# Expert weights in one ring of eighteen places, three experts in a loop's body, and waits moved behind the first output stores

## What is computed

```python
logits = xt @ w_router + b_router
top_v, top_e = lax.top_k(logits, 4)
weights = jax.nn.softmax(top_v, axis=-1)
def expert_block(tok, e):
    hcat = x_pad[tok] @ w1[e] + b1[e]                    # w1[e]: 1024 x 2048
    x_glu = jnp.minimum(hcat[:, ::2], 7.0)
    x_lin = jnp.clip(hcat[:, 1::2], -7.0, 7.0)
    act = x_glu * jax.nn.sigmoid(1.702 * x_glu) * (x_lin + 1.0)
    return act @ w2[e] + b2[e]                           # w2[e]: 1024 x 1024
out = sum over a token's four experts of weights * expert_block
```

## Time and profile before

| what | value |
|---|---|
| median of 3 runs | 2680.3 us (2677.91, 2680.3, 2681.9) |
| the profiled execution's own time | 2677.67 us |
| its span, first to last instruction | 2675.9 us |
| PE, DVE, ACT busy | 98%, 42%, 25% of the span |
| queue of SP's and ACT's loads | 664.71 MB of 705.21 MB |
| granted clock of TensorE, mean | 0.999 |

### The profile page before, as it was taken

One profiled execution on the slowest core, in us unless ns is written; L12 is line 12 of the kernel. 1 busy time (PEld: TensorE's weight loads), 2 busy tenths in 40 slices (PEclk: granted clock), 3 DMA queues, 4 the chain that ended last, 5 costly groups with the idle time before them and its releaser, 6 DMA issues.

```text
span 2675.9 us, 37947 instructions
## 1 busy us (share of the span) xinstructions
PE 2620.0 (98%) x15345; PEld 1908.5 (71%) x15345; DVE 1116.0 (42%) x1589; ACT 676.8 (25%) x1201; POOL 73.4 (3%) x95
## 2 busy tenths in 40 slices
PE   7999999999999999999999999999999999999998
PEld 7999888999999998899989888843333333333333
DVE  5866424586587463157823153322122112112212
ACT  3413320342143042213412044122121121112111
POOL 0010200000000120000001000000000000000000
PEclk9999999999999999999999999999999999999999
DMA  6575334456655843334562634779999999999999
GB/s 233 189 263 192 126 126 151 149 173 219 238 174 185 294 164 123 130 142 158 181 206 99 235 130 157 283 291 427 427 428 427 428 428 427 427 428 428 428 427 404
DMA packets 265069, 705.21 MB, mean 264 GB/s; under 512 B 12932, under 2 KB 155216, under 8 KB 214928
## 3 DMA queue, kind: packets, MB, share of 16 engines
q1 hardware_dynamic: 254464, 664.71, 64.5%
q0 software_dynamic: 9856, 36.41, 3.8%
q10 hardware_dynamic: 656, 2.78, 0.3%
HBM read 699.61 MB, written 6.60 MB: 264 GB/s over the span
## 4 chain that ended last, share of the span: by engine, by line
PE 78%; DMA 16%; SPq 4%; DVE 1%; issue 0%; ACT 0%; DVEq 0%; ACTq 0%
PE acc L1005 12%; PE acc L1093 11%; PE acc L1716 7%; PE acc L1050 6%; PE mix L1054 6%; PE acc L1052 6%; DMA ring<-in_w 6%; DMA branch<-in_w 5%; DMA big<-in_w 5%; PE acc L1532 4%; PE mix L1044 4%; PE acc L1731 3%; PE acc L1022 3%; SPq L881 2%; PE acc L1324 2%; SPq L884 2%
## 5 line engine op out<-in xcount | busy, mean ns | idle before, releaser
L1050 PE MATMUL acc<-branch_parts,area_parts 128*128 128x256 f32 x1176 | 344.1, 293 | 0.1
L1054 PE MATMUL mix<-big_parts,zz_parts 128*128 128x256 f32 x1176 | 332.8, 283 | 0.0
L1052 PE MATMUL acc<-area_parts,ring_parts 128*128 128x256 f32 x1176 | 332.4, 283 | 0.0
L1093 PE MATMUL acc<-big,ring 128*128 128x256 f32 (+1 forms) x1408 | 269.7, 353 | 0.0
L1093 PEld LDWEIGHTS acc<-big,ring 128*128 128x128 f32 x1408 | 241.1, 190 | 28.3 <-issue 0.8
L3012 DVE COPY zz<-acc 128x512 f32<-128x512 f32 x32 | 22.1, 691 | 555.9 <-PE acc L1716 555.9
L1050 PEld LDWEIGHTS acc<-branch_parts,area_parts 128*128 128x128 f32 x1176 | 225.0, 191 | 8.9 <-DVE zz_parts L2354 0.5
L1052 PEld LDWEIGHTS acc<-area_parts,ring_parts 128*128 128x128 f32 x1176 | 225.1, 191 | 0.2
L1054 PEld LDWEIGHTS mix<-big_parts,zz_parts 128*128 128x128 f32 x1176 | 225.0, 191 | 0.0
L1005 PE MATMUL acc<-x,ring 128*128 128x256 f32 x1024 | 224.3, 380 | 0.0
L1005 PEld LDWEIGHTS acc<-x,ring 128*128 128x128 f32 x1024 | 193.8, 190 | 26.7 <-issue 0.3
(11 more groups left out here) (506 smaller groups left out, 3667.1 us busy)
## 6 DMA issues: line engine op xcount, KB each, us to landing
big<-in_w SPq DMA_DIRECT2D x129, 1024.0 KB, 25.7
ring<-in_w SPq DMA_DIRECT2D x124, 1024.0 KB, 25.7
ring<-in_ffn_up SPq DMA_DIRECT2D x88, 1024.0 KB, 4.9
ring<-in_w_in SPq DMA_DIRECT2D x72, 1024.0 KB, 7.0
tables<-in_w SPq DMA_DIRECT2D x33, 1024.0 KB, 25.7
branch<-in_w SPq DMA_DIRECT2D x33, 1024.0 KB, 26.0
silu_rope<-in_w SPq DMA_DIRECT2D x31, 1024.0 KB, 25.7
res<-in_w SPq DMA_DIRECT2D x31, 1024.0 KB, 25.4
```

The source lines that it names most:

```text
L1050: pe.matmul(abank(a, b)[:, ts], wg[:, b, k, c * P:c * P + P], xg[:, k, :], start=c == 0 and k == 0, stop=False, skip_group_check=True)
L1052: pe.matmul(abank(a, b)[:, ts], wl[:, k, c0:c0 + P], xl[:, k, :], start=False, stop=k == K - 1, skip_group_check=True)
L1054: mm = pe.matmul(kbank(a, b)[:, ts], wk[:, b, k, c * P:c * P + P], xk[:, k, :], start=False, stop=k == K - 1, skip_group_check=True)
L1093: mm = pe.matmul(outs[c], w[:, k, c * P:c * P + P], rhs(kk), start=opens[c] and kk == 0, stop=kk == FC - 1, skip_group_check=not all(opens))
```

## The change

The constant `NWB` goes from 12 to 18, and unit u now lies in place u mod 18 throughout, so the six additional places are refilled like the others. As 18 places and 12 units an expert meet again only after three experts, the loops over experts 2 to 31 on SP and on PE run ten times over a body of three experts. The wait for the three loads of a next round stands before the fourth store instead of before the first. `first_units` loads all eighteen first units, at the same points in SP's stream as before. The diff's core:

```diff
-NWB = 12
+NWB = 18
...
-        w_landed = [sem(f"w_landed_{n}") for n in range(NWB)]
+        w_landed = [sem(f"w_landed_{n}") for n in range(12)]
...
-        def buffer_of(j):
-            return (8 + j - NX) % NWB
...
+        BUFFERS = tuple((w, 0) for w in w_landed) + \
+            ((small_landed, LAYERS * 176), (apart_landed, LAYERS * 48), (down_landed, LAYERS * 64), (const_landed, 64),
+             (rows_moved, 32), (landed[0], (LAYERS * (RINGED // 2) + 9) * 16))
...
         def laps(n):
-            return 1 + len([u for u in range(NWB + NX, UNITS_Q) if (u - NX) % NWB == n])
...
+            return len(range(n, UNITS_Q, NWB))
...
+        def unit_of(eng, q, u, i=0):
+            sem_n, counted = BUFFERS[u % NWB]
+            eng.wait_ge(sem_n, (q * laps(u % NWB) + 2 * i + (u // NWB + 1)) * 16 + counted)
+            return wbuf[u % NWB]
...
-                spare_units(NWB, NWB + NX - 1)
+                first_units(q, 12, 17)
...
-                spare_units(NWB + NX - 1, NWB + NX)
+                first_units(q, 17, 18)
...
-                def stream(e, first, last):
-
+                def stream(e, u, first, last):
...
                     for j in range(first, last):
-                        turn = NX if isinstance(e, int) and number(e, j) < 2 * NWB + NX else 0
-                        sp.wait_ge(w_used, q * UNITS_Q + e * UNITS_E + (j - 14 - turn))
+                        sp.wait_ge(w_used, q * UNITS_Q + e * UNITS_E + (j - 20))
                         if j < DC:
-                            up_unit(e, j, buffer_of(j))
+                            up_unit(e, j, (u + j) % NWB)
                         else:
-                            down_unit(e - 1, j - DC, buffer_of(j))
-
-                stream(1, 4 + NX, UNITS_E)
-                stream(2, 0, UNITS_E)
-                with sp.Fori(3, EXPERTS) as e:
-                    stream(e, 0, UNITS_E)
+                            down_unit(e - 1, j - DC, (u + j) % NWB)
+
+                stream(1, 8, 10, UNITS_E)
+                with sp.Fori(0, (EXPERTS - 2) // 3) as i:
+                    for d in range(3):
+                        stream(i * 3 + (2 + d), 20 + UNITS_E * d, 0, UNITS_E)
...
-            for n in range(3):
-                sp.wait_ge(w_landed[n], rounds * (16 * laps(n)) + 16)
             for i, n in enumerate((0, 2, 1, 3)):
+                if i == 3:
+                    for m in range(3):
+                        sp.wait_ge(w_landed[m], rounds * (16 * laps(m)) + 16)
                 sp.wait_ge(x_ready, 16 + 48 * LAYERS + 16 + i + 1)
...
-                with pe.Fori(2, EXPERTS) as e:
-                    slots_free(first + e)
-                    up(e, 0, 2)
-                    combine(first + e - 2)
...
+                with pe.Fori(0, (EXPERTS - 2) // 3) as i:
+                    for d in range(3):
+                        e, u = i * 3 + (2 + d), 20 + UNITS_E * d
+                        slots_free(first + e)
+                        up(u, 0, 2, i)
+                        combine(first + e - 2)
...
+                        down_between(e, u + DC, i)
```

More of the change, by code:

```diff
@@ L567, in mixed_blocks @@
         mask_ready = sgu_out
-        w_landed = [sem(f"w_landed_{n}") for n in range(NWB)]
+        w_landed = [sem(f"w_landed_{n}") for n in range(12)]
         w_used = sem("w_used")
[L572 to L580, removed]
-        def buffer_of(j):
-            return (8 + j - NX) % NWB
-        def last_unit(n):
-            return max(u for u in range(NWB + NX, UNITS_Q) if (u - NX) % NWB == n)
-        def laps(n):
-            return 1 + len([u for u in range(NWB + NX, UNITS_Q) if (u - NX) % NWB == n])
[L592 to L604, removed]
+        BUFFERS = tuple((w, 0) for w in w_landed) + \
+            ((small_landed, LAYERS * 176), (apart_landed, LAYERS * 48), (down_landed, LAYERS * 64), (const_landed, 64),
+             (rows_moved, 32), (landed[0], (LAYERS * (RINGED // 2) + 9) * 16))
+        THREE = 3 * UNITS_E
+        def laps(n):
+            return len(range(n, UNITS_Q, NWB))
[3 more added lines that the diff above has]
+            return wbuf[u % NWB]
         sel_ready = sem("sel_ready")
@@ L872, in _ @@
             w2 = io["w2_2"].rearrange("l e (k p two) c -> p (l e k) (two c)", p=P, two=2)
-            def landing(n):
-                return w_landed[n] if n < NWB else SPARE[n - NWB][0]
             def up_unit(e, k, n):
-                sp.dma_start(wbuf[n].unsqueeze(1), w1[:, bass.ds(e * DC + k, 1), :]).then_inc(landing(n), 16)
+                sp.dma_start(wbuf[n].unsqueeze(1), w1[:, bass.ds(e * DC + k, 1), :]).then_inc(BUFFERS[n][0], 16)
             def down_unit(e, k, n):
[L884 to L892, removed]
+                sp.dma_start(wbuf[n].unsqueeze(1), w2[:, bass.ds(e * 4 + k, 1), :]).then_inc(BUFFERS[n][0], 16)
             def first_units(q, a, b):
                 for n in range(a, b):
-                    up_unit(n // DC, n % DC, n)
+                    if n < 2 * DC:
+                        up_unit(n // DC, n % DC, n)
+                    else:
+                        down_unit(0, n - 2 * DC, n)
             for n in range(13):
@@ L1705, in combine, with up_unit @@
                 mm.then_inc(combined, 1)
[L1707 to L1713, removed]
+            def up_unit(q, k, u, i=0):
+                w = unit_of(pe, q, u, i)
                 for j in range(4):
@@ L1720, in up_unit, with down_unit @@
                 mm.then_inc(w_used, 1)
-            def down_unit(q, e, j):
-                w = unit_of(pe, q, e, j + (DC if not isinstance(e, int) or e < EXPERTS else 0)).rearrange("p (k c) -> p k c", k=2)
+            def down_unit(q, j, u, i=0):
+                w = unit_of(pe, q, u, i).rearrange("p (k c) -> p k c", k=2)
                 for kk in range(2):
@@ L1761, in up_first, with up @@
                         pe.wait_ge(x_slot_ready, first * DC + (k + 1))
-                        up_unit(q, None, k)
-                def up(e, a, b):
+                        up_unit(q, k, k)
+                def up(u, a, b, i=0):
                     for k in range(a, b):
-                        up_unit(q, e, k)
+                        up_unit(q, k, u + k, i)
                 def slots_free(it):
@@ L1799, in _ @@
                 slots_free(first + 1)
-                up(1, 0, 4)
+                up(8, 0, 4)
                 gather(first + 3)
-                up(1, 4, 6)
+                up(8, 4, 6)
                 gather_turn(first + 3)
-                up(1, 6, 8)
-                down_between(1)
-                with pe.Fori(2, EXPERTS) as e:
-                    slots_free(first + e)
-                    up(e, 0, 2)
-                    combine(first + e - 2)
[L1810 to L1815, removed]
+                up(8, 6, 8)
+                down_between(1, 16)
+                with pe.Fori(0, (EXPERTS - 2) // 3) as i:
[4 more added lines that the diff above has]
+                        combine(first + e - 2)
+                        up(u, 2, 4, i)
+                        gather(first + e + 2)
+                        up(u, 4, 6, i)
+                        gather_turn(first + e + 2)
+                        up(u, 6, 8, i)
+                        down_between(e, u + DC, i)
                 combine(first + (EXPERTS - 2))
```

20 lines of the change are left out of this document (10 added, 10 removed).

## The result

Five runs of the changed kernel gave 2667.07 us in the median (2666.69 to 2668.06), five of the kernel before, with the three of the first table among them, 2681.49 us (2677.91 to 2682.26). The ratio is 0.995, with a 95% interval of 0.9935 to 0.9964: 14.4 us or 0.5% faster. The forecast was 2666.7, in a range from 2662.5 to 2674.

The account below looks back on a forecast made before the run. The DMA streaming weights was taken to bound the expert stage. Closing its gap (12.2 us) and earlier stores (1.4 us) gave 13.6 us off, from a median of 2680.3 to 2666.7 us, range 2662.5 to 2674.

Parts of the forecast that it names:

- The bound: Expert stage: it ends when the DMA has moved its bytes, PE has 42.9 us to spare, only DMA-idle time can be won.
- The ring, 12.2 us: Refilling all eighteen places keeps SP's load queue fed from about 1782 to 1810 us: 12.2 us won, between 9.7 and 12.5.
- Whole of it reaches the end: All 12.2 us reach PE's last combine; the DMA stays the bound and PE waits for it from about 2200 us.
- account of 30.7 us of spare time: PE's chain of 792.0 us against the DMA's 822.7 with the gap closed, counted over the whole stage.
- Depth beyond the gap is worth nothing: In the DMA-bound part the queue takes only 10 to 11 units, so SP stands in the issue instead: no gain.
- Three experts in a body, nothing: PE's longer loop body, 804 records plus waits, taken as zero; stalls up to 3.1 us a turn covered by spare time.
- Rival 1: Each turn of PE's longer loop waits for an instruction fetch, making the kernel slower, at about 2688 us; chance 0.08.
- The tail, 1.4 us: At the end three stores go out before the last next-round load lands, the fourth 1.4 us earlier; floor zero, ceiling 2.0.
- The sum: Over the whole kernel, 12.2 + 1.4 = 13.6 us off, for a median of 2666.7 us, 0.51% faster.

Follow-up runs that it names:

- ring of fifteen: Changed kernel with fifteen places in the ring, the last three used once, and five experts in PE's body: 2672.05 us, ratio 0.9971 to the kernel before.
- 17 us of more work: Changed kernel with the gather's eight matmuls done twice for one expert in three: 2667.53 us, ratio 0.9953 to the kernel before.
- depth 12 from 2269 us on: Changed kernel, but from SP's seventh loop body on SP waits for the unit twelve back instead of eighteen: 2667.9 us, ratio 0.9954 to the kernel before.
- body alone: Kernel before, still with twelve places, with three experts in a body on PE and SP and nothing else: 2680.24 us against 2680.1.
- the gather done twice for all: Changed kernel with the gather's matmuls done twice for every expert of the loop, 51.6 us more PE work: 2685.61 us, ratio 1.0023 to the kernel before.

## Why the prediction was right, point by point

*The bound.* Right. In the stage only the time in which the DMA moved nothing could be won, and the ring of fifteen shows the gain following that time.

*The ring, 12.2 us.* Right in kind, about 1 us too high: 11 us by the stages (12.0 by the pair of profiles that the forecast starts from, 10 to 12 over all). The bounds were 9.7 and 12.5. The refill went as worked out: the `spare` pair is issued at 1780.83, which is 1778.4 on the clock of the trace before, the windows hold 424 and 426 GB/s, and zp, area and tn are refilled twenty times each. The gap itself was sized rightly. The weights' queue from 32 to 100 us after the stage's start, before (1778.33 to 1846.33) and after (1780.79 to 1848.79):

```profile
q1 hardware_dynamic: 3246, 23.59, 84.8%
...
q1 hardware_dynamic: 3971, 28.90, 100.8%
```

These 5.31 MB are 12.4 us. The missing 1 us lies in the first 32 us of the stage, which the forecast let stand: there the queue moved 11.27 to 11.40 MB in the three profiles with twelve places, and 10.60 to 11.13 in the eight with eighteen, 0.5 MB or 1.2 us less in the mean. The shortest stages are those with the most (11.13 MB: 908.7; 11.01: 909.3), the longest those with the least (10.60: 910.8). Why less comes in there with eighteen places isn't shown.

*Whole of it reaches the end.* Right. PE's first wait came at 2205.53, forecast near 2200 (in other profiles up to some 40 us earlier and 20 later). The account of 30.7 us of spare time held in both directions: 17 us of more work were free, and 50 us cost 18, for a forecast of 19.

*Depth beyond the gap is worth nothing.* Right: landing as before, SP longer in the issue, and depth 12 from 2269 us on the same time.

*Three experts in a body, nothing.* Right: body alone 1.0 (0.9991 to 1.0009). I had said no packets after 1840; there were two by 1900, in the first pass, and none after. Rival 1, the fetch at each turn, didn't happen with bodies of three and of six experts, 804 and 1608 records. The Trainium skill's page "Runtime: NRT & Kernel Launch" (instruction fetch mechanics) has two rules on this. Its room for 2048 instructions on PE agrees with all three lengths, if a record is an instruction: 1608 leave 440 for their waits, and over 4000 don't fit. Its window of two pages of 256 instructions, outside which the target of a taken branch is fetched first, does not agree for PE, since 804 and 1608 records are more than 512 and no turn fetched.

*The tail, 1.4 us.* Right: 1.5. The three profiles with the wait before the first store have 8.87 to 9.02, those with it before the fourth 7.32 to 7.48, and 7.01 with the gather done twice for all, where PE ends last.

*The sum, and how far one profile goes.* The forecast for the difference was 13.6; the medians differ by 14.4, the two profiled spans by 11.0, and when the changed kernel was timed again it was 12.0. The parts, 11 and 1.5, make 12.5. So that the forecast median was missed by only 0.4 us is in part luck. Most of the 3.4 us between the spans and the medians is there because the stage began 2.46 us later in the one after. I looked for a cause in the change and found none: 0.8 us are there from well before it, and the rest comes in the twelve microseconds from 1720. The kernel before:

```profile
1720.00:1724.00 4.00, 4.00 (x30) 3.91 (x30) 0.00 (x0) 0.44 (x1) 0.00 (x0) 0.81 1.01 420
1724.00:1728.00 4.00, 4.00 (x15) 3.32 (x15) 0.00 (x0) 0.64 (x2) 0.00 (x0) 0.76 1.01 426
1728.00:1732.00 4.00, 4.00 (x24) 3.56 (x22) 0.29 (x1) 0.00 (x0) 0.00 (x0) 1.00 0.96 406
```

and the changed one, with the same work in these windows:

```profile
1720.00:1724.00 4.00, 4.00 (x30) 4.00 (x30) 0.00 (x0) 0.00 (x0) 0.00 (x0) 0.76 1.02 424
1724.00:1728.00 4.00, 4.00 (x14) 3.46 (x13) 0.00 (x0) 1.08 (x2) 0.00 (x0) 0.50 1.01 428
1728.00:1732.00 4.00, 4.00 (x18) 3.46 (x17) 0.00 (x0) 0.00 (x0) 0.00 (x0) 0.89 1.01 424
```

The granted clock (the third number from the right) is below full here. A window whose mean is 0.50 was at the lower level, 1.2 GHz, throughout, so the time at that level is (0.19 + 0.24) x 4 / 0.5 = 3.4 us before and (0.24 + 0.50 + 0.11) x 4 / 0.5 = 6.8 us in the changed kernel. At half speed half of that is lost: 1.7 and 3.4 us, and the difference of 1.7 is the rest of the 2.46. PE worked without a gap ahead of it in both, so what sets the length of the fall isn't shown. The other twelve-place profiles start the stage at 1748.3 and 1749.9, so it was the profile before that was early. The forecast's working against the profile's own time, and then its difference taken to the median, was the right way round; a comparison of two single spans would have said 11.

## What to carry to other kernels

Where a stage streams more than the compute can use, look for the windows in which the stream stands still, ask which buffer the next load waits for, and add places just there: the time won is the dry time, not a share of the stage, and the three places of six that filled about 60% of the missing bytes won about two thirds of the time. Count the slower partner's spare time as an account over the whole stage, with the lead that the stream has at its start, and not as a difference of rates: 29.03 against 29.43 us per expert looked free and cost 18 us. And when the change is half a per cent, read each trace from the start of the stage that changed, since what comes before may move by as much as the thing sought.

## What the runs showed of the hardware that was not expected

SP's queue, once full, held some 10 to 12 loads of 1 MB (landing 25 to 29 us after issue, at 2.45 us each), with twelve places as with eighteen; further issues hold SP for mostly 1.89 and up to 5.8 us. A body of 1608 matmul and load records on PE ran in a loop with no instruction packet after its first pass; one of over 4000 fetched 29 packets of 16 KB, and while it did the weights' queue moved 1.11 MB less for 0.48 MB of packets, and the stage took 5.3 us more, which is twice what the missing bytes account for; near the end the sixteen DMA engines no longer finished together.
